# A two-layer mixture-of-experts trunk: router logits by token, the norm's weight on gathered rows, unread products, and the first expert pair in halves

## What is computed

```python
xn = rms_norm(h, ln_ffn[l])                  # h * rsqrt(mean(h*h) + eps) * gain
h = h + hier_moe(xn, ...)

def hier_moe(xt, w_rg, b_rg, w_re, b_re, w_gate, w_up, w_down):
    g_logits = xt @ w_rg + b_rg              # 4 groups; the best one is taken
    e_logits = (xt @ w_re + b_re)            # 8 experts in it; the best two are taken
    ...
    for e in range(N_EXPERTS):
        hid = silu(xt @ w_gate[e]) * (xt @ w_up[e])
        y = y + combine[:, e:e + 1] * (hid @ w_down[e])
```

## Time and profile before

| | us |
|---|---|
| median of 3 runs | 1200.93 (1200.26 to 1201.15) |
| the profiled execution | 1200.14 |
| its span, first to last instruction | 1198.3 |
| PE busy | 1126.8 (94%) |
| DVE / ACT / POOL busy | 221.0 / 233.7 / 115.6 |
| moved | 444 MB, mean 371 GB/s |
| mean granted clock of TensorE | 0.993 |

### The profile page before, as it was taken

How to read it: one execution, slowest core, us unless ns; L and a number is a source line. 1 busy time by engine, 2 the same in 40 slices (tenths; PEclk the granted TensorE clock), 3 DMA queues, 4 the chain that set the end, 5 groups by cost and what they waited for, 6 DMA issues and landing times.

```text
span 1198.3 us, 13942 instructions
## 1 busy us (share of the span) xinstructions
PE 1126.8 (94%) x4998; PEld 504.3 (42%) x4998; DVE 221.0 (18%) x581; ACT 233.7 (20%) x546; POOL 115.6 (10%) x307
## 2 busy tenths in 40 slices
PE   8999989999999988889999999899999998888897
PEld 6776543333333332223387755333333332222232
DVE  2765350000000000000223234400000000000002
ACT  2144131111121111111112232311121111111111
POOL 0002111100011000000000000200001000000001
PEclk9999999999999999999999999999999999999999
DMA  6984589999999999999998364899999999999994
GB/s 237 336 349 180 215 311 398 427 421 428 428 428 428 429 429 429 428 426 428 423 368 330 106 229 173 313 418 429 418 429 427 429 428 428 428 428 428 428 428 190
DMA packets 49450, 444.33 MB, mean 371 GB/s; under 512 B 9660, under 2 KB 14840, under 8 KB 17656
## 3 DMA queue, kind: packets, MB, share of 16 engines
q1 hardware_dynamic: 48040, 441.34, 88.8%
q10 hardware_dynamic: 1360, 2.31, 0.6%
HBM read 442.54 MB, written 1.09 MB: 370 GB/s over the span
## 4 chain that ended last, share of the span: by engine, by line
PE 65%; DMA 29%; DVE 4%; issue 1%; ACT 1%; SPq 0%; POOL 0%; POOLq 0%; ACTq 0%; DVEq 0%
PE PS L1534 23%; PE PS L1543 12%; DMA places<-in_moe_w_up 12%; DMA places<-in_moe_w_gate 11%; PE PS L1284 8%; PE PS L1550 6%; DMA places<-in_moe_w_down 6%; PE PS L1416 5%; PE PS L1288 4%; PE PS L1296 1%; PE PS L1371 1%; PE PS L1503 1%; PE PS L1400 1%; PE PS L1601 1%; PE PS L1585 1%
## 5 line engine op out<-in xcount | busy, mean ns | idle before, releaser
L1534 PE MATMUL PS<-places,mix 128*64 128x512 f32 x1984 | 442.1, 595 | 43.4 <-DMA places<-in_moe_w_up 29.5
L1534 PEld LDWEIGHTS PS<-places,mix 128*64 128x64 f32 x1984 | 142.3, 137 | 335.1 <-issue 281.2
L1543 PE MATMUL PS<-places,gain_att 128*64 128x512 f32 x960 | 215.1, 599 | 4.0 <-ACT gain_att L809 3.5
L1550 PE MATMUL PS<-mix 128*128 128x512 f32 x256 | 124.8, 608 | 0.0
L1543 PEld LDWEIGHTS PS<-places,gain_att 128*64 128x64 f32 x960 | 66.4, 137 | 129.8 <-issue 124.9
L762 ACT ACTIVATE mix<-acts 128x512 f32 x120 | 76.3, 636 | 226.6 <-PE PS L1534 214.3
L1284 PE MATMUL PS<-acts,places 128*128 128x256 f32 x448 | 103.2, 384 | 0.0
L1185 DVE TENSOR_TENSOR mix<-PS,mix 128x512 f32<-128x512 f32 x30 | 20.7, 692 | 426.2 <-PE PS L1534 418.0
L1284 PEld LDWEIGHTS PS<-acts,places 128*128 128x128 f32 x448 | 83.2, 190 | 14.9 <-issue 3.1
L527 POOL TENSOR_TENSOR sm<-sm 128x1 f32<-128x1 f32 x32 | 6.2, 193 | 697.6 <-PE PS L1608 697.5
L566 POOL TENSOR_SCALAR mix<-drop 128x64 f32<-128x64 f32 x128 | 72.0, 579 | 0.0
(11 more groups left out here) (218 smaller groups left out, 626.1 us busy)
## 6 DMA issues: line engine op xcount, KB each, us to landing
places<-in_moe_w_gate SPq DMA_DIRECT2D x56, 2048.0 KB, 25.1
places<-in_moe_w_down SPq DMA_DIRECT2D x54, 2048.0 KB, 32.5
places<-in_moe_w_up SPq DMA_DIRECT2D x52, 2048.0 KB, 30.3
places<-in_moe_w_gate SPq DMA_DIRECT2D x16, 1024.0 KB, 10.2
places<-in_moe_w_up SPq DMA_DIRECT2D x16, 1024.0 KB, 6.2
places<-in_moe_w_down SPq DMA_DIRECT2D x16, 1024.0 KB, 8.1
places<-in_c_w_in SPq DMA_DIRECT2D x12, 1024.0 KB, 20.5
places<-in_ab_w_in SPq DMA_DIRECT2D x8, 1024.0 KB, 13.8
```

The source lines that it names most:

```text
L1534: last = mm(PS[e * SLOTS:(e + 1) * SLOTS, 2 + part, :], xg[:, k, e * SLOTS:(e + 1) * SLOTS], w[e][:, kk, :], start=(k == 0), stop=(k == NK ...
L1543: last = mm(PS[e * SLOTS:(e + 1) * SLOTS, 6 + b, :], hidT[:, k, e * SLOTS:(e + 1) * SLOTS], w[e][:, 512 * b:512 * b + 512], start=(k == 0) ...
L1550: last = mm(PS[:, Y_BANK[q]], pickT[:, t], ye[:, 512 * b:512 * b + 512], start=first, stop=final)
```

## The change

1. `route` multiplies `xT`, now the stationary operand, with the router's weights; the logits come out by token, and ACT's copy and `route_back` are gone.
2. `rescaled` is gone. ACT makes `xn` = h * rstd (one pass per tile); the norm's weight `ln_ffn` is put on when gathered rows leave PSUM, as a scale per partition: in ACT's copies of the tile 0 gather (eight instead of four), in `first_ranges` (the first copy of a bank is two now) and in DVE's copies of the tile 1 gather, which become products. The two loads of `ln_ffn` are gone, and one load of a weight chunk waits no longer for `rescaled`.
3. After the second tile's ranks PE makes three products that nobody reads.
4. `first_pair`: pair 0 works in halves; its picks are transposed behind the first down chunk. ACT turns to SiLU without waiting for `s_go`, and copies the hidden values before the next pair's columns. `passes` on DVE comes after the copy of the turned picks.

The core of the diff:

```diff
@@ -489,7 +491,6 @@
                     chunk(l, 1, 1, m)
                 sp.wait_ge(s_ss, 2 * (2 * l + 1) + 2)
                 chunk(l, KEPT, KEPT, OUT_CHUNKS)
-                sp.wait_ge(s_xn, NT * l + 2)
                 chunk(l, KEPT, KEPT, OUT_CHUNKS + 1 + IN_BIAS)
                 for c in range(OUT_CHUNKS, CHUNKS):
                     sp.wait_ge(s_used[l], used_before(1, c))
...
                     if t:
                         counts_copy(0)
-                    act.wait_ge(s_lT, NT * l + t + 1)
-                    act.activation(logT[0:ROUTES, t], PS[0:ROUTES, 6 + t, 0:P], ACT.Copy).then_inc(s_lc, 1)
+                    act.wait_ge(s_rs, 2 * (2 * l + 1) + t + 1)
+                    act.activation(xn[:, t], h[:, t], ACT.Copy, scale=rstd[:, t:t + 1]).then_inc(s_xn, 1)
                     if t == 0:
                         exps_of(0)
 
                 def gathered_copy(b):
 
                     act.wait_ge(s_g, NK * l + b + 1)
-                    act.activation(sorted_x[0][:, b * 512:(b + 1) * 512], PS[:, GATHER_BANK[0][b]], ACT.Copy).then_inc(s_xa, 1)
+                    for kk in range(PER_BANK):
+                        k = b * PER_BANK + kk
+                        ins = act.activation(sorted_x[0][:, k * SEQ:(k + 1) * SEQ], PS[:, GATHER_BANK[0][b], kk * SEQ:(kk + 1) * SEQ], ACT.Copy,
+                                             scale=ffn_gain(l, k))
+                    ins.then_inc(s_xa, 1)
 
...
                         bank = PS[:, GATHER_BANK[1][b]]
                         act.wait_ge(s_g, NK * l + NK // PER_BANK + b + 1)
                         act.wait_ge(s_xg[l], 3 * b + 1)
-                        act.activation(dst(to0, ks), bank.rearrange("p (b n) -> p b n", b=PER_BANK)[:, :, 0:SLOTS], ACT.Copy).then_inc(s_xg[l], 1)
+                        for kk in range(PER_BANK):
+                            k = b * PER_BANK + kk
+                            ins = act.activation(mix[:, bass.ds(to0 + k * AREA, SLOTS)], bank[:, kk * SEQ:kk * SEQ + SLOTS], ACT.Copy,
+                                                 scale=ffn_gain(l, k))
+                        ins.then_inc(s_xg[l], 1)
...
                         for kk in range(PER_BANK):
                             ins = act.activation(mix[:, bass.ds(to1 + (b * PER_BANK + kk) * AREA + SLOTS, SLOTS)],
-                                                 bank[:, bass.ds(second1 + kk * SEQ, SLOTS)], ACT.Copy)
+                                                 bank[:, bass.ds(second1 + kk * SEQ, SLOTS)], ACT.Copy, scale=ffn_gain(l, b * PER_BANK + kk))
                         ins.then_inc(s_xg[l], 1)
 
                 def experts(i, first=False, final=False):
                     if not final:
                         entries = [entries_of(i + 1, e) for e in range(AT_ONCE)]
                     act.wait_ge(s_used[l], i * CHUNKS + UP_CHUNKS)
-                    if not first:
-                        act.wait_ge(s_ht[l], i)
+                    if first:
+                        act.wait_ge(s_wt, l + 1)
+                    else:
+                        act.wait_ge(s_ht[l], i + 1)
                     act.activation(hid, PS[:, 2], ACT.Silu).then_inc(s_si[l], 1)
-                    if not final:
+                    if not first and not final:
 
                         act.wait_ge(s_used[l], i * CHUNKS + 2 * UP_CHUNKS)
...
-                    for half in range(2 if final else 0):
+                    for half in range(2 if first or final else 0):
                         ks = slice(half * NF // 2, (half + 1) * NF // 2)
-                        act.wait_ge(s_ht[l], i + 1 + half)
+                        act.wait_ge(s_ht[l], i + (1 if first else 2) + half)
                         act.activation(hidT[:, ks], PS[:, 2 + half, half * F // 2:(half + 1) * F // 2].rearrange("p (k n) -> p k n", k=NF // 2),
                                        ACT.Copy).then_inc(s_hT[l], 1)
+                    if first:
+                        ranges(entries, FIRST_COPIES)
                     if final:
                         act.wait_ge(s_left, l + 1)
+                    elif first:
+                        act.wait_ge(s_used[l], CHUNKS)
                     else:
-                        act.wait_ge(s_ht[l], i + 1)
+                        act.wait_ge(s_ht[l], i + 2)
...
                 second1 = act.value_load(tables[0:1, 2, 1:2], min_val=0, max_val=P)
                 first_ranges(to0, first1, to1, second1)
                 act.activation(sm[:, 126:127], half[:, 0:1], ACT.Silu)
-                act.wait_ge(s_go[l], 1)
                 experts(0, first=True)
                 for n in range(1, ROUND):
                     experts(n)
+                act.wait_ge(s_go[l], 1)
                 if l + 1 == DEPTH:
                     act.wait_ge(s_used[l], KEPT * CHUNKS + OUT_CHUNKS + ONCE)
-                    load_gain(DEPTH)
...
 
-            def rescaled(l, t):
-
-                dve.wait_ge(s_h, 4 * l + 2 * t + 2)
-                dve.wait_ge(s_rs, 2 * (2 * l + 1) + t + 1)
-                dve.wait_ge(s_gain, 16 * (l + 1))
-                dve.scalar_tensor_tensor(xn[:, t], h[:, t], rstd[:, t:t + 1], gain, ALU.mult, ALU.mult).then_inc(s_xn, 1)
-
...
 
                 dve.wait_ge(s_g, NK * l + NK // PER_BANK + b + 1)
                 dve.wait_ge(s_xg[l], 3 * b + 4)
-                dve.tensor_copy(sorted_x[1][:, b * 512:(b + 1) * 512], PS[:, GATHER_BANK[1][b]]).then_inc(s_xd, 1)
+                ks = (DEPTH + l) * NK + b * PER_BANK
+                dve.tensor_tensor(sorted_x[1][:, b * 512:(b + 1) * 512].rearrange("p (k n) -> p k n", k=PER_BANK),
+                                  PS[:, GATHER_BANK[1][b]].rearrange("p (k n) -> p k n", k=PER_BANK),
+                                  gain_col[:, ks:ks + PER_BANK].unsqueeze(2).broadcast_to((P, PER_BANK, SEQ)), ALU.mult).then_inc(s_xd, 1)
 
             dve.memset(drop0[:, :], 0.0).then_inc(s_blank, 1)
...
                 turn_copy(l + 1, 0)
-                rescaled(l, 0)
+                dve.wait_ge(s_ss, 2 * (2 * l + 1) + 1)
...
                 picks(l, 0)
-                rescaled(l, 1)
                 route(l, 1)
...
-                passes(l)
-
-                def experts(i, final=False):
+
+                def experts(i, first=False, final=False):
                     dve.wait_ge(s_used[l], i * CHUNKS + 2 * UP_CHUNKS)
                     dve.wait_ge(s_si[l], i + 1)
-                    if final:
+                    if first or final:
                         for half in range(2):
                             fs = slice(half * F // 2, (half + 1) * F // 2)
                             dve.tensor_tensor(hid[:, fs], PS[:, 3, fs], hid[:, fs], ALU.mult).then_inc(s_hi[l], 1)
                     else:
                         dve.tensor_tensor(hid, PS[:, 3], hid, ALU.mult).then_inc(s_hi[l], 1)
                     dve.wait_ge(s_pkt[l], i + 1)
-                    dve.tensor_copy(pickT, PS[:, 2 if final else 3, 0:NT * P].rearrange("p (t n) -> p t n", t=NT)).then_inc(s_pkT[l], 1)
+                    dve.tensor_copy(pickT, PS[:, 0 if first else 2 if final else 3, 0:NT * P].rearrange("p (t n) -> p t n", t=NT)).then_inc(s_pkT[l], 1)
+                    if first:
+                        passes(l)
                     dve.wait_ge(s_used[l], i * CHUNKS + CHUNKS)
                     dve.tensor_copy(ye[:, 512:1024], PS[:, 7]).then_inc(s_yd[l], 1)
 
-                experts(0)
+                experts(0, first=True)
                 experts(1)
...
-                    last = mm(PS[0:ROUTES, 6 + t, 0:P], wr[:, k, :], xT[:, k, t * P:(t + 1) * P], start=(k == 0), stop=(k == NK - 1))
+                    last = mm(PS[:, 6 + t, 0:ROUTES], xT[:, k, t * P:(t + 1) * P], wr[:, k, :], start=(k == 0), stop=(k == NK - 1))
                 if NK - 1 in ks:
-                    last.then_inc(s_lT, 1)
-
-            def route_back(l, t):
-
-                pe.wait_ge(s_lc, NT * l + t + 1)
-                nc.tensor.transpose(PS[:, 6 + t, P:P + ROUTES], logT[0:ROUTES, t], ident[0:ROUTES, 0:ROUTES]).then_inc(s_lg, 1)
+                    last.then_inc(s_lg, 1)
 
             def ranks(l, t):
 
...
                 mm(PS[:, 4, o:o + EXPERTS], ones, chose_before[:, t, EXPERTS:2 * EXPERTS], start=False, stop=True).then_inc(s_rk, 1)
+                if t:
+                    pe.wait_ge(s_known, NT * l + t)
                 mm(PS[:, 5, o:o + 2 * EXPERTS + 1], ones, chose_before[:, t], start=True, stop=True).then_inc(s_rk, 1)
 
             def gather(l, t, banks=range(NK // PER_BANK)):
...
+                def first_pair():
 
                     for c in range(2 * UP_CHUNKS):
+                        up_chunk(0, True, 0, 0, c)
+                    for half in range(2):
+                        pe.wait_ge(s_hi[l], 1 + half)
+                        for k in range(half * NF // 2, (half + 1) * NF // 2):
+                            last = nc.tensor.transpose(PS[:, 2 + half, k * P:(k + 1) * P], hid[:, k * P:(k + 1) * P], ident)
```

(17 more changed lines are left out.)

61 lines of the change are left out of this document (28 added, 33 removed).

## The result

The changed kernel takes 1191.35 us (median of 4 runs, 1189.84 to 1192.72) against 1200.60 us (1199.25 to 1201.15): a ratio of 0.9926, 95% interval 0.9913 to 0.9938. In a second set it was 1190.99 against 1199.95 us, 0.9927 (0.9913 to 0.9941). So the change is worth about 9 us, where 5.7 were forecast and 7.0 were the most that the forecast's bounds gave. The profiled execution took 1190.6 us, its span is 1188.8 us.

A forecast was written before the change was run, and what follows sets the result against it. It took transfer time lost in holes before the long 426 GB/s stretches, ended by PE's path to pair 0, as the bound. 1.6 + 1.9 + 1.9 + 0.3 = 5.7 us gave 1195.2 us, range 1192.8 to 1197.8.

The forecast's parts named there:

- What bounds the kernel: Both layers: transfers missed in holes before the long 426 GB/s stretches decide; PE's path to pair 0 ends the holes.
- Logits by token: Routing: ACT's copy, turned product and DVE's scaling leave the path; 0.3 plus 1.0, 1.3 us (0.9 to 1.5).
- The norm's weight: Gathered rows: four scaled copies on the path cost 0.3 to 0.4 us per layer; ACT's 1.15 us pass fills a wait.
- late 128x512 copy in layer 0: Layer 0 routing: ACT's already late copy ahead of the second gather's first copy slips, costing 0.3 us (0 to 0.8).
- Unread products: Behind the second tile's ranks: they keep the clock up in the second gather, gaining 0.95 us per layer.
- Rival (a): Routing: the clock falls all the same, costing 0.95 us per layer; 1197.1 us, dear form 1199.9; chance 0.13.
- The place: Pair 0's first up chunk is used and its place freed earlier, by 1.6 us in layer 0, 1.9 in layer 1.
- First pair: Pair 0 in halves: second down chunk some 3 us sooner in layer 0; worth 1.9 us there, 0.3 in layer 1.
- (b): Only the first hole shrinks, the second stays open for its own reason; 3.5 us gained, 1197.4 us; chance 0.10.
- (c): Router: 128-column weights cost 0.1 us for each of 16 products per layer; 2.5 us gained, 1198.4 us; chance 0.03.
- (d): Nothing reaches the end: transfers take the gain back in the long stretch; 1200.9 us; chance 0.04.
- (e): Ahead of the first expert product: ACT's pass and scaled copies become the bound; 1203.1 us, slower; chance 0.04.

The follow-up runs named there:

- e12: Kernel before with only the logits made straight by token, DVE's scaling kept; 1196.82 us, ratio 0.9979.
- e7: Changed kernel with the logits made by experts and turned back as before, DVE's scaling still gone; 1194.22 us, ratio 0.9955.
- e8: Changed kernel with ACT's copies out of the gathers plain, ACT's part of the norm's weight left out; 1191.87 us, ratio 0.9928.
- e14: Kernel before with only the three unread products added between the second tile's ranks and its gather; 1198.35 us, ratio 0.9993.
- e2: Changed kernel run again with no edit, for a second trace; 1190.99 us, ratio 0.9927.
- e4: Changed kernel with four more unread 128x128 products at its start, while PE waits for the first loads; 1193.53 us, ratio 0.9946.
- e5: Changed kernel with the first pair of layer 1 alone whole, as it was before; 1195.04 us, ratio 0.9966.
- e6: Changed kernel with the first pair of layer 0 alone whole, as it was before; 1193.70 us, ratio 0.9948.
- e10: Changed kernel with one more unread 128x256 product per layer, ahead of the second half of the second tile's router products; 1190.85 us, ratio 0.9930.
- e1: Kernel before run again with no edit, for a second trace; 1199.88 us, ratio 0.9997.
- e9: Kernel before with only the new first pair (halves, copies first, table of passes and turned picks later); 1193.99 us, ratio 0.9958.
- e13: Kernel before with five unread 128x256 products in the first pair of each layer, nothing else changed; 1197.86 us, ratio 0.9990.
- e11: Kernel of e10 without the three unread products behind the ranks; 1192.55 us, ratio 0.9942.

## Why the prediction came out low

**What bounds the kernel** was right in its main point: transfers missed before the long stretches decide, and the rate after them stays at 427 GB/s. One sentence of it was wrong: PE does not wait for weights from 188 to 390 us. The earlier trace rows has PE busy for 202.00 of 202.00 us, with the DMA engines full as well; the profile shows no wait of PE for a load there. It waits only behind 390 us, in the kernel before:

```profile
390.00:552.00 162.00, 141.99 (x614) 49.00 (x612) 9.73 (x16) 22.32 (x37) 14.76 (x40) 1.00 1.01 428
```

The likely reason is that PE works through a stock of loaded chunks first; no run tests it. A microsecond of an earlier load was also not quite a microsecond of transfer: 3.22 us brought 2.75.

**Logits by token**: forecast 1.3 us per layer for ACT's copy, the turned products and DVE's scaling, measured 1.62 and 1.63. The second tile's part was right, 1.0 us forecast and 0.97 measured. The first tile's part was too small, 0.3 us forecast: the second half of the second tile's router products starts 0.65 us earlier, counted from the load ahead of the routing (149.08 - 110.39 against 146.62 - 108.58). That the three must leave together is right as well (e12). The products with 128 columns of weights cost nothing to see: 1.08 us for the eight records at 146.62 us where the old form took 1.06, and for the first tile's sixteen the next product even follows sooner (1.70 us, against 1.86 in e7).

The 2.5 us per layer estimated from the Trainium skill (TensorE: Matmul & The Clock Gate, LDWEIGHTS) did not appear. The weight loads themselves are as far apart as the Trainium skill's section says: the traces have a mean of 113 ns for those of 36 columns (L1477, before) and 191 ns for those of 128 (L1480, changed), 78 ns more where its rule gives 77. They lie beside the products, though, and did not lengthen them.

**The norm's weight**: 0.35 us forecast, 0.38 measured (e8), 1.15 us for the pass (L730) as worked out. The 0.3 us for a late 128x512 copy in layer 0 did not come: it starts ahead of the second gather, after 0.84 us of waiting (153.68 and 153.94 us).

**Unread products**: the size of a fall in the second gather was right, 0.95 us (e14: 0.94 and 0.95), and they held the clock in it in 18 of 18 cases. That they hold it in the whole routing was too sure: of the seven traces with them in the changed routing order and the narrow router products (changed, e2, e4, e5, e6, e8, e10), three fall at about 149 us in the first gather (1.0 to 1.1 us) and one at 739 us in layer 1 (1.06 us). Rival (a) was thus half true in four of seven traces, by a fall ahead of the products. I had foreseen a fall around the ranks only.

**The place** came 2.23 and 2.19 us earlier, where 1.6 and 1.9 were forecast. The parts add up to it: 1.62 - 0.38 + 0.95 = 2.19. The shortfall of the forecast is the first tile's 0.35 us in both layers, and the 0.3 us for ACT's late copy in layer 0.

**First pair**: here the sum failed most, by 0.85 us in layer 0 and 0.95 in layer 1 or more. In layer 0 the second load moved by 3.22 us (some 3 forecast), and 2.75 us of transfers came back (2.80 to 0.05) where I took 1.9. In layer 1 I took 0.3 us, from one stretch of 4 us at 377 GB/s. The miss went on for 20 us around it, at 411 GB/s (0.79 us), and came again 80 us later (0.65 us): 1.25 us more in all than in the changed kernel. And in two of the five traces with an unfilled, whole first pair in layer 1 (e1 and e14; not before, e5 and e12) the clock fell in its down phase as it had in layer 0, which makes it 3.2 to 3.3 us. The step that failed is "since layer 1 loses 4 x (1 - 377 / 426) = 0.5 us with its load issued in time, I take 1.9 us for layer 0 and 0.3 for layer 1": the load was not in time, it was 1.7 us later than it could be (21.91 against 20.23 us), and the loss does not end with the 4 and 5 us of the two holes.

**The sum anew**: layer 0 place 2.2 (1.1 with the fall at 149), layer 1 place 2.2, first pair 2.75 to 3.2 in layer 0 and 1.25 to 3.2 in layer 1: 8.4 us with the falls of the first trace of each kernel, 7.3 to 10.8 with others; the medians give 9. In the terms of the forecast's sum, 5.7 became 8.4: 0.6 and 0.3 us more at the place, 0.85 and 0.95 more at the first pair. By marks in the traces, layer 0 from the load at 110 us to the one at 705 us went from 595.12 to 591.50 us (3.6 us; forecast 3.5, by a gain of 5.0 of which over 1 us is lost again at the layer's end, where one load landed 1.2 us late; e4 and e10, with 591.24 and 590.93, keep some more of it), and the rest went from 492.82 to 488.70 (4.1 us; forecast 2.2, by the marks 3.4). Together that is 7.7 us behind the start, and e1 against e2 gives 7.7 as well. Three things are open: why layer 0's end gives back about 0.6 us even in e10, why layer 1 gains 0.7 us more than its two marks, and why the medians are 1.3 to 1.5 us further apart than the traces.

**Rivals**: (b), (c), (d) and (e) did not come. ACT is not what the first product waits for by more than the four scales: PE idles 1.00 us ahead of it, and 0.61 us in e14, where the copies are plain and the clock stays up as well. The difference is 0.39 us.

## What to carry to other kernels

Where transfers are the limit, read their rate over a window that takes in the whole disturbance, and look again one turn of the ring later: a late release of a place cost once at the load and, in eight of the twelve cases here, once more 80 us later. A clock that falls in one trace is a draw, not a constant; take two traces of the kernel before ahead of costing an edit that shortens an idle time, and price every gap after which the clock can fall. An edit that keeps the clock up in one gap does not do it for the next: e14 had its fall 21 us behind the gather that it had mended. And count the stretch of interest over all traces at hand, whatever they were taken for; the second gather's 18 of 18 against 3 of 14 said more than any median.

## What the runs showed of the hardware

The granted clock fell to its lower level with PE hardly idle: at 149.2 us in e2 PE had waited 0.39 us, and what ran ahead of it were router products 36 wide and rank products 32 to 65 wide; with router products 128 columns wide on the moving side it did not fall there. Of the ten traces with the narrow form (changed, e2 to e6, e8, e10 to e12) four have a fall at the start of layer 0's first gather and one (e6) in layer 1's, of the six with the wide one (before, e1, e7, e9, e13, e14) none in either; in e10 and e11 a wide product stood among them, and neither fell. Over both layers that is 5 of 20 against 0 of 12: a hint, and not shown. What a fall costs depends on what runs in it: 1.7 us on the first gather cost the place 1.1 us (PE had idled 0.36 us ahead of the ranks behind it), and 1.7 us on the second cost it 0.95.

The runs of one kernel differ by 2 to 6 us, and their mean granted clock mostly goes with the time: of the 17 runs of before beside e9 to e12, the three under 1198 us had 0.995 or 0.996, the two above 1201 us 0.991 and 0.992. Not always: the slowest of e10's six, 1193.48 us, had 0.997, no less than its fastest.
